# Experts of a decoder layer: rows of tokens stationary, gate-up put together from pieces of 32, 64, 64 and 128 rows

## What is computed

```python
logits = t @ router_w + router_b                 # t: 1024 tokens x 1024
top_logit, top_idx = lax.top_k(logits, 4)        # 4 of 32 experts for each token
gates = softmax(top_logit)
gu = t[tok] @ w_gate_up[e] + b_gate_up[e]        # 1024 -> 2048, columns gate, up, gate, up, ...
gate = minimum(gu[:, 0::2], 7.0)
up = clip(gu[:, 1::2], -7.0, 7.0)
act = (up + 1.0) * gate * sigmoid(1.702 * gate)
y = act @ w_down[e] + b_down[e]                  # 1024 -> 1024
out = segment_sum(y * gate_of_token)
```

## Time and profile before

| | |
|---|---|
| median of 3 runs | 3578.26 us (3578.1 to 3587.09) |
| profiled execution, its own time | 3584.87 us |
| its span, first to last instruction | 3583.2 us |
| mean granted TensorE clock | 0.914 of full speed |
| PE busy | 3009.2 us (84%) |
| PE weight loads busy | 2197.5 us (61%) |
| DVE, ACT, POOL busy | 1207.4, 608.9, 182.8 us |
| instruction queue | 156 packets, 2.56 MB |

### The profile page before, as it was taken

The page is one execution under the profiler, slowest core; times in us unless marked ns, Lnnn a source line. Parts: engine busy times, 40 slices in busy tenths (PEclk is TensorE's granted clock), DMA queues, the critical chain, the costliest instruction groups (busy, mean ns, idle before and its releaser), DMA issues.

```text
span 3583.2 us, 47317 instructions
## 1 busy us (share of the span) xinstructions
PE 3009.2 (84%) x15924; PEld 2197.5 (61%) x15925; DVE 1207.4 (34%) x3431; ACT 608.9 (17%) x1547; POOL 182.8 (5%) x188
## 2 busy tenths in 40 slices
PE   3577746999985997499999999999999898999991
PEld 1244426666652564477777777777876686777770
DVE  1155440667762554222222222222222222222224
ACT  0011110555551332000100010100010010000110
POOL 0000000000000001000000000000000000000000
PEclk8788875999997996699999999999999999999995
DMA  3522132333004110665544585566876565645835
GB/s 107 186 51 50 39 70 56 93 80 80 13 6 137 36 42 18 244 231 207 189 164 164 184 292 209 206 230 217 286 266 226 193 234 176 239 156 179 285 119 241
DMA packets 306091, 555.10 MB, mean 155 GB/s; under 512 B 80350, under 2 KB 115422, under 8 KB 304840
## 3 DMA queue, kind: packets, MB, share of 16 engines
q1 hardware_dynamic: 265912, 509.39, 42.0%
q0 software_dynamic: 21152, 38.50, 3.1%
q10 hardware_dynamic: 18832, 4.33, 0.6%
HBM read 525.89 MB, written 70.93 MB: 167 GB/s over the span
## 4 chain that ended last, share of the span: by engine, by line
PE 52%; issue 3%; DVE 2%; DVEq 1%; ACTq 1%; ACT 1%; DMA 0%; POOL 0%; POOLq 0%
PE ps L1635 34%; PE ps L1653 16%; PE ps L1658 2%; DVE x L1604 1%; PE ps L1617 1%; ACT xT_e L1521 0%; ACTq L1421 0%; DVE gg L1572 0%; DMA d_ys<-ys_e,dst 0%; DVEq L1421 0%; DVEq L1424 0%; DMA xg<-d_h,src 0%; DVE ys_e L1589 0%; DVEq L1557 0%; ACT ss L1540 0%
## 5 line engine op out<-in xcount | busy, mean ns | idle before, releaser
L1635 PE MATMUL ps<-xT_e,wg 128*128 128x128 f32 (+2 forms) x8192 | 1249.1, 316 | 35.5 <-issue 32.4
L1635 PEld LDWEIGHTS ps<-xT_e,wg 128*128 128x128 f32 x8192 | 1208.8, 197 | 91.4 <-issue 53.3
L1653 PE MATMUL ps<-wd,aT 128*128 128x512 f32 x1248 | 568.4, 612 | 11.3 <-issue 9.3
L1653 PEld LDWEIGHTS ps<-wd,aT 128*128 128x128 f32 x1248 | 239.3, 196 | 321.3 <-issue 321.3
L1572 DVE TENSOR_SCALAR gg<-ps,bias 128x128 f32<-128x128 f32 (+2 forms) x256 | 101.3, 396 | 713.0 <-PE ps L1635 712.9
L1540 ACT ACTIVATE ss<-gg 128x128 f32<-128x128 f32 (+2 forms) x256 | 88.7, 346 | 895.5 <-DVE gg L1572 895.2
L1540 ACT ACT_TABLE_LOAD x32 | 41.1, 1283 | 880.0 <-issue 880.0
L428 PE MATMUL ps<-w_in,hT_a 128*128 128x430 f32 x512 | 187.8, 529 | 0.0
L723 PE MATMUL ps<-ident_t,sc 128*128 128x128 f32 x880 | 150.2, 287 | 31.6 <-ACT sc L789 28.2
L789 ACT ACTIVATE sc<-sc,nm 128x640 f32<-128x640 f32 (+15 forms) x256 | 161.6, 634 | 68.4 <-DVE nm L831 68.4
L1589 DVE COPY ys_e<-ps 128x1024 f32<-128x1024 f32 x22 | 26.3, 1222 | 421.9 <-PE ps L1658 218.1
(11 more groups left out here) (290 smaller groups left out, 2588.2 us busy)
## 6 DMA issues: line engine op xcount, KB each, us to landing
wg<-in_w_gate_up SPq DMA_DIRECT2D x128, 2048.0 KB, 8.1
wd<-in_w_down SPq DMA_DIRECT2D x128, 1024.0 KB, 4.9
wg<-d_ys SPq DMA_DIRECT2D x8, 2048.0 KB, 10.8
d_bias<-d_rev SPq DMA_DIRECT2D x1, 10368.0 KB, 41.0
w_in<-in_w_in SPq DMA_DIRECT2D x1, 6880.0 KB
x_a<-in_x POOLq DMA_DIRECT2D x8, 512.0 KB, 8.5
kn<-d_kn SPq DMA_DIRECT2D x8, 512.0 KB
strip_t<-d_bias SPq DMA_DIRECT2D x8, 512.0 KB
```

The lines of the kernel that those rows point to most:

```text
L1635: mm = pe.matmul(ps[:, j % 2, half * PASS:half * PASS + w], wg[:, j // 2, k, c0:c0 + 255:2], xT[:, k, 0:w], start=(k == 0), stop=(k == KD ...
L1653: mm = pe.matmul(ps[:, 2 + 2 * b + h, :], aT[:, j, b * P:b * P + r], wd[:, c, j % 2, h * 512:(h + 1) * 512], start=(j == 0), stop=(j == JD ...
```

## The change

TensorE now holds the rows still and moves the weights, 512 columns at a time. Gate-up is put together from four pieces of code: q (32 rows), g (64), h (64) and f (128 rows). Rows 0 to 127 are f, 128 to 191 h, 192 to 223 q, or 192 to 255 g. With up to 96 rows they lie from 128 on. Seven sizes result (`ARMS`): 64 h, 96 qh, 128 f, 160 qf, 192 hf, 224 qhf, 256 ghf. TensorE chooses by flags in the plan, the other engines by size (`by_rows`). A piece of 64 rows uses the two halves of the array for two chunks of weights, a piece of 32 rows the four quarters for all four chunks. So q reads every chunk in its one unit.

The output now has rows on the partitions. The bias is a row, loaded for each pass by a DMA that repeats it on 128 partitions. The activations (`aa`) have to be transposed on TensorE (`turn_act`) and copied by ScalarE (`copy_act`) ahead of down; the last of each piece is turned inside down (`last_turn`). `wd` is laid out so that each partition holds two neighbouring rows. `bgT` and its setup are gone, VectorE no longer loads `expert`, the plan has eight numbers for a pass, and the credit of the semaphores is 16, not 8.

```diff
-CREDIT = 8
+CREDIT = 16
...
-                sp.dma_start(ident[:, :], e.c_ident).then_inc(s_in, 16)
-                sp.dma_start(bgu[:, :], e.b_gate_up[0]).then_inc(s_in, 16)
...
+                step(dve.tensor_scalar(over[:, 0, :], steps[:, 0, :], r[:, 6:7], None, ALU.is_lt))
+                step(dve.tensor_tensor(steps[:, 1:4, :], steps[:, 1:4, :], bcast(over[:, 0:1, :], [P, 3, 7]), ALU.mult))
+                step(dve.tensor_reduce(r[:, 7:10], steps[:, 1:4, :], AX.X, ALU.add))
...
+        SEG = {"q": (P // 4, 192, 1), "g": (P // 2, 192, 2), "h": (P // 2, 128, 2), "f": (P, 0, 4)}
+        BANK = {"q": (1,), "g": (0, 1), "h": (0, 1), "f": (0, 1, 0, 1)}
+        ACT_BANK = {"q": (2,), "g": (2, 4), "h": (3, 7), "f": (6, 7, 6, 7)}
+        ARMS = {64: "h", 96: "qh", 128: "f", 160: "qf", 192: "hf", 224: "qhf", 256: "ghf"}
...
                         for c in range(NCH):
-                            sp.wait_ge(s_gu, CREDIT + JD * i + 2 * (c + 1) - JD)
+                            sp.wait_ge(s_gu["h"], CREDIT + 2 * i + c // 2 + 1 - 2)
+                            hold(sp, e.sp_passed)
+                            sp.wait_ge(s_gu["f"], CREDIT + 4 * i + c + 1 - 4)
...
+                        for k in "qghf":
+                            sp.wait_ge(s_rd[k], CREDIT + SEG[k][2] * i)
+                            hold(sp, e.sp_passed)
+                        sp.dma_start(bias[:, :], e.b_gate_up[0][one, :].rearrange("o n -> (o n)").partition_broadcast(P)).then_inc(s_bias, 16)
...
+                def copy_act(i, k, j):
+                    kind, t0, per = SEG[k]
+                    act.wait_ge(s_aT[k], CREDIT + per * i + j + 1)
+                    groups = P // kind
+                    out = aT[:, 2 * j * groups:2 * (j + 1) * groups, t0:t0 + kind].rearrange("p (g f) n -> p f g n", f=2)
+                    act.activation(out, ps[:, ACT_BANK[k][j], 0:2 * P].rearrange("p (f g n) -> p f g n", f=2, n=kind), ACT.Copy).then_inc(s_aTc[k], 1)
...
+                                for m, (k, j) in enumerate(units(rows)):
+                                    act.wait_ge(s_g, CREDIT + U * i + upto(rows, m))
+                                    act.activation(ss[:, :], gg[:, :], ACT.Sigmoid, scale=ALPHA).then_inc(s_sig, count(rows, m))
+                                    if k == "f" and j:
+                                        copy_act(i, "f", j - 1)
+                                for k, j in (("q", 0), ("g", 0), ("g", 1), ("h", 0)):
+                                    if k in ARMS[rows]:
+                                        copy_act(i, k, j)
+                            by_rows(act, n, sigmoids)
+                            next_rows(i + 1, after)
...
+                                for g in range(groups):
+                                    read = dve.tensor_tensor(gu[part, :], ps[part, BANK[k][j], :], bias[part, cols], ALU.add)
+                                read.then_inc(s_rd[k], 1)
+                                dve.tensor_scalar(gg[:, :], gu[:, 0::2], LIMIT, None, ALU.min).then_inc(s_g, add)
+                                dve.tensor_scalar(uu[:, :], gu[:, 1::2], LIMIT, -LIMIT, ALU.min, ALU.max).then_inc(s_u, add)
+                                dve.scalar_tensor_tensor(vv[:, :], uu[:, :], 1.0, gg[:, :], ALU.add, ALU.mult).then_inc(s_v, add)
+                                dve.tensor_tensor(aa[:, AA[k][j], :], vv[:, :], ss[:, :], ALU.mult).then_inc(s_a[k], 1)
...
+                        def unit(k, j):
+                            kind, t0, per = SEG[k]
+                            groups = P // kind
+                            for c in range(j * groups, (j + 1) * groups):
+                                loaded(c)
+                            for kk in range(KD):
+                                for g in range(groups):
+                                    mm = pe.matmul(ps[g * kind:(g + 1) * kind, BANK[k][j], :], xT[:, kk, t0:t0 + kind], wg[:, j * groups + g, kk, :],
+                                                   start=(kk == 0), stop=(kk == KD - 1))
+                            mm.then_inc(s_gu[k], 1)
...
+                            for j in range(4):
+                                unit("f", j)
+                                if j:
+                                    pe.wait_ge(s_a["f"], CREDIT + 4 * i + j)
+                                    turn_act("f", j - 1)
...
+                        def last_turn(k, j):
+                            pe.wait_ge(s_a[k], CREDIT + SEG[k][2] * i + SEG[k][2])
+                            pe.wait_ge(s_xTc, CREDIT + 4 * i + 4 + 3)
+                            turn_act(k, j)
+                            pe.wait_ge(s_aTc[k], CREDIT + SEG[k][2] * i + SEG[k][2])
+
+                        def whole(b, turn):
+                            for c in range(NCH):
+                                pe.wait_ge(s_wd[c], CREDIT + 16 * i + 16)
+                                if c == 2:
+                                    last_turn(*turn)
+                                for h in range(2):
+                                    for j in (2 * c, 2 * c + 1):
+                                        mm = pe.matmul(ps[:, 2 + 2 * b + h, :], aT[:, j, b * P:(b + 1) * P], wd[:, c, j % 2, h * 512:(h + 1) * 512],
+                                                       start=(j == 0), stop=(j == JD - 1))
+                                mm.then_inc(s_down[b], 1)
```

More of the change, by code:

```diff
@@ L1413, in stage_experts @@
         s_wd = [sem(f"e_wd{c}") for c in range(NCH)]
[L1414 to L1415 removed]
+        s_bias, s_g, s_u, s_v, s_sig = (sem("e_" + n) for n in ("bias", "gate", "up", "product", "sigmoid"))
+        s_gu, s_rd, s_a, s_aT, s_aTc = ({k: sem(f"e_{n}_{k}") for k in "qghf"} for n in ("gate_up", "gate_up_read", "act", "actT", "actT_copied"))
@@ L1442, in by_blocks, with units, absent @@
-        def by_blocks(eng, n, body):
-            with eng.If(n > P):
-                with eng.If(n > P + P // 2):
-                    body((P, P))
-                with eng.Else():
-                    body((P, P // 2))
-            with eng.Else():
-                body((P,))
+                by_rows(eng, n, body, sizes[:half])
+        def units(rows):
+            return [(k, j) for k in ARMS[rows] for j in range(SEG[k][2])]
+        def absent(rows):
+            return [k for k in "qghf" if k not in ARMS[rows]]
@@ L1452, in stage_experts, with upto, count @@
+        def upto(rows, m):
+            return U if m == len(units(rows)) - 1 else m + 1
+        def count(rows, m):
+            return U - m if m == len(units(rows)) - 1 else 1
         with nc.Block() as block:
@@ L1596, in _ @@
-                        by_blocks(dve, n, evict)
+                            first = "f" in ARMS[rows]
+                            if first:
+                                dve.wait_ge(s_down[0], CREDIT + NCH * i + NCH)
+                                take(0, 2, 1 if len(ARMS[rows]) > 1 else 2)
+                            if ARMS[rows] != "f":
+                                dve.wait_ge(s_down[1], CREDIT + NCH * i + NCH)
+                                take(int(first), 4, 1 if first else 2, halves=rows in (64, 160, 192))
@@ L1598, in _ @@
+                        by_rows(dve, n, evict)
                 for t in range(NT):
@@ L1613, in turn_rows @@
                         pe.wait_ge(s_xTc, CREDIT + 4 * i + max(k - 1, 0))
+                        if k == 1 and busy is not None:
+                            pe.wait_ge(s_aTc["f"], busy)
                         for kk in range(2):
@@ new lines, in none @@
+                        def none(k):
+                            pe.sem_inc(s_gu[k], SEG[k][2])
+                            pe.sem_inc(s_aT[k], SEG[k][2])
+                        with pe.If(hasq > 0):
+                            unit("q", 0)
+                        with pe.Else():
+                            none("q")
+                        with pe.If(hasg > 0):
+                            unit("g", 0)
+                            unit("g", 1)
+                        with pe.Else():
+                            none("g")
@@ new lines, in _ @@
+                        with pe.Else():
+                            none("f")
+                        pe.wait_ge(s_y, CREDIT + 2 * i)
+                        hold(pe, e.pe_passed)
+                        with pe.If(hasq > 0):
+                            pe.wait_ge(s_a["q"], CREDIT + i + 1)
+                            turn_act("q", 0)
+                        with pe.If(hasg > 0):
+                            for j in range(2):
+                                pe.wait_ge(s_a["g"], CREDIT + 2 * i + j + 1)
+                                turn_act("g", j)
@@ L1643, in _ @@
-                        pe.wait_ge(s_a, CREDIT + JD * i + JD)
-                        pe.wait_ge(s_y, CREDIT + 2 * i)
-                        def down(rows):
+                            turn_rows(i + 1, 1, CREDIT + 4 * i + 3)
+                        pe.wait_ge(s_aTc["f"], CREDIT + 4 * i + 3)
```

(4 more changed lines are left out.)

279 lines of the change are left out of this document (157 added, 122 removed).

## The result

| | before | after |
|---|---|---|
| median of the runs | 3578.18 us (3572.3 to 3587.09) | 3740.98 us (3739.92 to 3742.97) |
| ratio | | 1.045, 95% interval 1.0432 to 1.0469 |
| span of the profiled execution | 3583.2 | 3739.7 |
| expert stage to TensorE's last matmul | 1479.2 to 3502.6: 2023 | 1474.7 to 3591.8: 2117 |
| tail, from there to the end | 81 | 148 |

The forecast was 3492, and faster: 249 us off, with the wrong sign. Against the forecast the stage is 169 us too long (1948 were forecast, 2023 - 200 - 21 + 146) and the tail 78 us (+67 instead of -11). First the page of after: its chain of waits, against the earlier trace rows, and the packets of the two instruction queues (packets, MB, share). Before, q14 had 39 packets and 0.32 MB, q8 156 and 2.56 MB.

A forecast was written before the change was run, and what follows sets the result against it. TensorE was taken to bound the expert stage. Gate-up -200, down -21, added path terms against the old gaps +146 and the loop -11 gave -86, so 3492 us against a median of 3578.26; range 3430 to 3580.

The forecast's parts named there:

- R3: Rival, gate-up: q's quarters run only two at a time, 14.4 us a unit, +144 us, 3636 us; chance 0.09.
- (a): From gate-up's end to down: the chain of activation, copies and transposes takes 4.6 us in each of 32 passes, 147 us.
- (b): `last_turn` inside down: two transposes and ScalarE's copy, for which TensorE waits, 42 times 1.4 us, 59 us.
- (c): `turn_act` inside f: 40 pairs at 0.25 us, 10 us.
- (g): DMA of weights, bias, gather and scatter at 388 GB/s: only passes of h wait, 5 us in all.
- R2: Rival, DMA: mixed traffic gives 330 GB/s, not 388, costing 52 us minus the 5 counted, 3539 us; chance 0.11.
- (d): Start of a pass: TensorE loads five plan values where it had two, no longer hidden behind down, 41 us (0 to 120).
- (e): Clock lost in the gaps ahead of down: 25 of the 32 gaps at 1.8 us, 45 us.
- R1: Rival, clock: it falls in every gap, 102 us instead of 45, 3549 us; chance 0.14.
- (f): TensorE's gate-up code shrinks, so far jumps miss only at first use, 20 us (0 to 128).
- R4: Rival, code: far jumps still miss once per pass with twelve branches, +108 us, 3600 us; chance 0.06.
- Tail: After the last pass: VectorE's walk over 15 empty passes gets 0.7 us shorter each, -11 us; next late, loads of `d_ys`.

The follow-up runs named there:

- e2: The changed kernel with a branch on the flag around each of TensorE's waits, so it waits only for pieces in the pass: 3552 us, ratio 0.992.
- e10: The kernel before with 180 never executed instructions put into VectorE's loop body: 3651 us, ratio 1.020.
- e11: The kernel before with 900 never executed instructions put into ScalarE's loop body: 3586 us, ratio 1.001.
- e15: The changed kernel with 64 never executed instructions on ScalarE ahead of its loop, which moves the loop by 69: 3668 us, ratio 1.024.
- e8: The kernel before with 400 never executed instructions put into VectorE's loop body: 3723 us, ratio 1.041.
- e3: The changed kernel with ScalarE's seven arms replaced by one branch per piece: 3784 us, ratio 1.057.
- e5: The changed kernel with ScalarE's seven arms replaced by one branch per piece, and one dummy Sigmoid at the start of each pass: 3673 us, ratio 1.026.

## Why the prediction was wrong

**Work: right.** Gate-up was forecast at 1035 us. In e2, where fewer gaps lower the clock, it is 1039.9 (568.7 + 328.0 + 143.2). A unit of f takes 7.03 from turn to turn, h 6.98, q 7.07 (but for one of 8.6 to 8.8). R3 is out: four quarters run at once with no loss. The 7.2 stood there without a row of four at once, so that it came out was in part luck. Down's unit is 14.0 as before.

**(a) Right:** 4.6 forecast; 4.0 to 6.0 in the 32 passes of the changed kernel, 4.9 in the mean, such as 5.2 (2063.7 to 2068.92 above). Their sum is 158 us, where 147 were forecast. **(b)** 1.4 each; 0.47 + 0.39 = 0.9 measured, so some 20 us better. **(c)** right, 0.23 each. **(g) Right:** TensorE waited 7.4 us for gate-up's weights, 5 were forecast. R2 is out.

**(d) Start of a pass, the step that failed in the stage.** I priced TensorE's five value loads and branches (41 us) and nothing else: the wait for absent pieces stood at nothing, without a reason. The waits on `s_rd` of absent pieces stand in the code ahead of h and f, and I counted no wait there. What was queued behind the waiting instruction was all of gate-up, and what it waited for was queued on VectorE behind the last copy of the pass before, a trip round the loop and a branch tree (in four passes the bias as well). It measured 219.5 us. With the waits gone (e2) the stage is 1919.7 us from 1474.7, against the 1948 of the forecast.

**(e) Clock:** 45 forecast for the gaps ahead of down. The gaps that came were at the start of gate-up, and the units behind them run at 15.7 to 16.7 us for 14.0; the stage's clock was 0.93, and 0.97 in e2. Gate-up's records are 28 us shorter there (1068 to 1040). This is a consequence of (d), not R1.

**(f) Code, the step that failed in kind.** For TensorE it was right: q8 fell from 156 to 47 packets. But the earlier trace rows stood for me for the engine that shows misses, and I read "L1437 on DVE stays near 50 ns" as a property of VectorE. It was one of its loop then, 307 instructions by the count above. The change took three arms from TensorE and put seven on VectorE and on ScalarE, 483 and 335 instructions. Nowhere did I count these. R4 had the mechanism on the wrong engine. The Trainium skill (Runtime: NRT & Kernel Launch, Instruction fetch mechanics) says that a taken branch whose target isn't in the current two-page window stalls for a fetch of that page, and that each engine has such a store; had I held it against every engine's loop, this rival would have been there. The trace agrees that branches stall, and e10 that no instruction has to be executed for it; that far jumps in e11 cost nothing is not what one window over neighbouring pages would give.

**Tail: half right.** VectorE's part came as forecast, 22.95 for about 20. "Next late would be the loads of `d_ys`" was the failed step: next late was ScalarE, 105 us behind the first sum. It walks the same 15 empty passes, and I had looked at that walk on VectorE only.

The error in sum: the stage of the changed kernel is 197 us longer than e2's (2117 and 1920). 190.5 of these are idle time ahead of gate-up (232.5 for 42.0) and 28 the shorter records of gate-up; less 21.5 that come up elsewhere when TensorE is earlier, 17.6 of them waits for activations. e2's stage is 28 us shorter than the forecast, which leaves 169. The other 78 are the tail, 76 of which e15 takes away (148 to 72).

What stays open: what exactly the instruction store keeps. ScalarE's empty pass is slow with a loop of 335 and of 467 instructions at one place, fast at another place (e15), and fast with 421 and 1021 in the kernel before. This shows that the place of the loop's head and end counts beside its length. The reading of four packets above fits, but isn't tested. VectorE's loop was only made longer, not moved.

## What to carry to other kernels

When branches go from one engine to another, count the loop body of each engine before and after; one that has no misses can have them when its body grows, even by code that it never runs (VectorE's from 259 to 441 instructions here). Do not let the busiest engine wait for a signal that something is absent: give it the flag, for here the signal came from the engine that was last to start the pass. An engine with nothing left to do still walks its empty passes, and if it issues the final stores, that walk is on the path.

## What the runs showed of the hardware that I had not expected

- Four 32-column pieces side by side run with no loss: 32 matmuls of 128x512 in 7.07 us, as long as 8 on the whole array (7.03).
- Never executed code in VectorE's loop: 182 instructions more cost 69 us in 32 passes (e10), 402 more 147 us (e8).
- The same loop 69 instructions further on: ScalarE's last of 15 empty passes 120 us earlier (3603.9 for 3723.6), an empty pass 1.8 us for 8.3.
- Beside the loads of `d_ys`, when the DMA moves 336 GB/s (3599 to 3649 us), an empty pass with missing code takes 15.8 to 17.4 us; behind them, at 5 GB/s, 8.0 to 8.5.
- Sigmoids and copies in branches of their own: 138 table loads of 1283 ns for 32 (e3), and one dummy call at the head brings them back to 32 (e5).
